# GpSimd's sums of squares wait until all eight chunks of a stage's input are split

## The reference

```python
def _rmsnorm(x, g):
    x32 = x.astype(jnp.float32)
    y = x32 * lax.rsqrt(jnp.mean(x32 * x32, axis=-1, keepdims=True) + RMS_EPS)
    return (y * g.astype(jnp.float32)).astype(x.dtype)
```

## Time and profile before

| what | value |
|---|---|
| time, median of 3 runs | 4003.52 us (4003.36 to 4012.45) |
| span of the profiled execution | 4004.4 us |
| PE busy | 3909.7 us, 98% |
| DVE busy | 2736.3 us, 68% |
| ACT busy | 1987.8 us, 50% |
| POOL busy | 212.2 us, 5% |
| mean granted clock of PE, of full speed | 0.991 |

### The profile page before, as it was taken

How to read it: one execution, slowest core, us unless ns; L and a number is a source line. 1 busy time by engine, 2 the same in 40 slices (tenths; PEclk the granted TensorE clock), 3 DMA queues, 4 the chain that set the end, 5 groups by cost and what they waited for, 6 DMA issues and landing times.

```text
span 4004.4 us, 78708 instructions
## 1 busy us (share of the span) xinstructions
PE 3909.7 (98%) x34150; PEld 3793.3 (95%) x34150; DVE 2736.3 (68%) x4071; ACT 1987.8 (50%) x2620; POOL 212.2 (5%) x277
## 2 busy tenths in 40 slices
PE   8999999999999999999999999999999999999999
PEld 8979999889998999999997999999998899999999
DVE  6566665666655656567555799956756699974855
ACT  5445444454544545465435545754444544764443
POOL 0011000110002000010023000000000000000000
PEclk9999999999999999999998999999999999999999
DMA  6534555345555455534550455456654455455754
GB/s 237 192 115 151 192 190 190 133 148 195 181 194 182 160 199 184 195 133 173 191 204 34 159 194 181 177 199 233 229 196 153 158 177 193 175 182 202 265 199 158
DMA packets 114791, 720.78 MB, mean 180 GB/s; under 512 B 13328, under 2 KB 13664, under 8 KB 32784
## 3 DMA queue, kind: packets, MB, share of 16 engines
q1 hardware_dynamic: 90144, 652.25, 45.9%
q10 hardware_dynamic: 19200, 37.01, 2.5%
q0 software_dynamic: 5104, 26.49, 1.9%
HBM read 692.48 MB, written 23.22 MB: 179 GB/s over the span
## 4 chain that ended last, share of the span: by engine, by line
PE 87%; DVE 7%; ACT 4%; issue 1%; POOL 0%; DMA 0%; ACTq 0%; DVEq 0%; POOLq 0%
PE psum L655 26%; PE psum L657 26%; PE psum L656 26%; PE psum L1408 3%; DVE slab_low L1916 2%; ACT slab_high L1427 2%; DVE h_parts L2219 1%; PE psum L1065 1%; PE psum L1048 1%; PE psum L875 1%; PE psum L1078 1%; ACT room L1670 1%; DVE room L2248 0%; DVE room L2253 0%; PE psum L1349 0%
## 5 line engine op out<-in xcount | busy, mean ns | idle before, releaser
L1916 DVE TENSOR_TENSOR slab_low<-slab,slab_high 128x2048 fp32r<-128x2048 f32 x622 | 1423.2, 2289 | 738.8 <-ACT slab_high L1427 736.6
L655 PE MATMUL psum<-h_parts,slab_high 128*128 128x256 f32 x5632 | 1578.2, 280 | 28.9 <-DVE h_parts L2219 18.6
L1427 ACT ACTIVATE slab_high<-slab 128x2048 fp32r<-128x2048 f32 x622 | 1189.3, 1912 | 785.4 <-PE psum L657 721.1
L656 PE MATMUL psum<-h_parts,slab_high 128*128 128x256 f32 x5632 | 1556.5, 276 | 0.0
L657 PE MATMUL psum<-h_parts,slab_low 128*128 128x256 f32 x5632 | 1556.1, 276 | 0.0
L655 PEld LDWEIGHTS psum<-h_parts,slab_high 128*128 128x128 f32 x5632 | 1063.5, 189 | 48.8 <-issue 24.0
L655 PE MATMUL psum<-hidden_parts,slab_high 128*128 128x256 f32 x3840 | 1063.5, 277 | 11.4 <-DVE hidden_parts L2166 4.8
L656 PEld LDWEIGHTS psum<-h_parts,slab_high 128*128 128x128 f32 x5632 | 1063.5, 189 | 2.4 <-issue 2.2
L657 PEld LDWEIGHTS psum<-h_parts,slab_low 128*128 128x128 f32 x5632 | 1062.8, 189 | 0.0
L656 PE MATMUL psum<-hidden_parts,slab_high 128*128 128x256 f32 x3840 | 1058.0, 276 | 0.0
L657 PE MATMUL psum<-hidden_parts,slab_low 128*128 128x256 f32 x3840 | 1058.0, 276 | 0.0
(11 more groups left out here) (346 smaller groups left out, 3326.0 us busy)
## 6 DMA issues: line engine op xcount, KB each, us to landing
slab<-in_up SPq DMA_DIRECT2D x176, 1024.0 KB, 4.8
slab<-in_keys_up SPq DMA_DIRECT2D x128, 1024.0 KB, 4.8
slab<-in_keys_down SPq DMA_DIRECT2D x128, 1024.0 KB, 4.8
slab<-in_down SPq DMA_DIRECT2D x88, 1024.0 KB, 4.8
slab<-in_w_in SPq DMA_DIRECT2D x16, 1024.0 KB, 4.8
slab<-in_wq SPq DMA_DIRECT2D x16, 1024.0 KB, 4.8
peer_gates<-room ACTq DMA_DIRECT2D x64, 256.0 KB, 2.3
room<-peer_gates ACTq DMA_DIRECT2D x64, 256.0 KB, 5.4
```

The source lines that it names most:

```text
L655: nc.tensor.matmul(out, lhs[0], rhs[0], start=first, stop=False, **options)
L656: nc.tensor.matmul(out, lhs[0], rhs[1], start=False, stop=False, **options)
L1427: nc.scalar.activation(k.high[m % PARTS][:, 0:width], k.slabs[m % RING][:, 0:width], ACT.Copy).then_inc(k.rounded.up())
L1916: nc.vector.tensor_tensor(k.low[m % RING][:, 0:width], k.slabs[m % RING][:, 0:width], k.high[m % PARTS][:, 0:width], ALU.subtract).then_in ...
```

## The change

GpSimd waits, once and ahead of its three additions, until `h_ready` stands at the eighth chunk of this stage. The three additions, what they read and the waits that they had stay, and so does the order of the instructions on every engine.

```diff
     def add_squares(self, v):
         k, nc = self.k, self.k.nc
+        nc.gpsimd.wait_ge(k.h_ready.sem, k.h_ready.at(DC))
         for j in range(DC // 2):
             nc.gpsimd.wait_ge(k.squared.sem, k.squared.at(j + 1))
             pair = v.square[:, 2 * j:2 * j + 2, :]
```

## The result

The changed kernel took **4035.69 us** (median of 5 executions, 4028.05 to 4038.91), the kernel before 4004.99 (median of 5 beside it): 1.007 times as long, 95% interval 1.006 to 1.008. That is +30.7 us, where +17 was forecast with 4009 to 4031 as the range: the sign was right, the size too small. Its eleven executions reach from 4020.5 to 4038.9 with a median of 4030.7, so about +25 is the better figure for what the change costs.

The account below looks back on a forecast made before the run. PE was taken to bound the kernel, with 87% of the chain. 4004.4 + 8.9 of waits (17.3 lost, 8.4 gained) + 8.2 of clock = 4021.5 us span, 0.9 less for the median: 4020.5 us, range 4009 to 4031.

Parts of the forecast that it names:

- What bounds, and what is removed: PE waiting for DVE's low parts: the eighth ready about 2.5 us sooner per stage, 8.4 us gained in four stages.
- The turns on DVE and GpSimd: Additions taking turns with DVE's slab subtractions make PE's sums late in six stages: 17.3 us lost, 6.8 in `stick`.
- PE's clock: Behind the new waits in six stages PE runs at 1.2 GHz for a while: 8.2 us lost, ends 0 and 15.
- From span to median: Whole kernel: the median lies 0.9 us below the span that was read, so 4021.5 becomes 4020.5 us.
- (1): PE's clock holds or its cost is hidden by later waits, so only the waits count: 4012.4 us, chance 0.22.
- (2): Clock costs 15 us, `mixer_one` 1.5 each, and `peer` loses its gain: 4032 us, chance 0.13.
- (3): Additions find DVE idle and sums are never late, so only the gain is left: 3995 us, chance 0.05.
- (4): Nothing happens, as additions always started after the eighth part, or gain and loss cancel: 4003.5 us, chance 0.03.

## Why the prediction was right, and where it failed

- **What bounds, and what is removed: right.** The four stages gained 8.6 us of 8.4 forecast. One sign for it was named wrongly: the idle time that low parts end was to lose most of its 18.6 us and lost 2.3. The view that groups waits tells why, of before and then of after:

```profile
PE psum L655 <- DVE h_parts L2219: 18.6, 10, 12.7
PE psum L655 <- DVE slab_low L1916: 10.0, 16, 1.2
```

```profile
PE psum L655 <- DVE h_parts L2219: 16.3, 5, 12.7
...
PE psum L655 <- DVE slab_low L1916: 3.3, 9, 1.0
```

12.7 of the 18.6 us are one wait, at the start of the program, which no edit of the stages moves; most of what fell, 6.7 us, was put down to the slab that DVE subtracts behind the low parts. The earlier trace rows names only the first releaser.
- **The turns on DVE and GpSimd: right in their sum,** 16.4 us of later sums for 17.3 forecast, `stick` to a tenth. One detail was wrong. In `stick` the addition that waited did not go ahead of DVE's next instruction, as at 17.83 in the earlier trace rows; DVE's second subtraction, back to back with the first, went ahead of it (4.48 us for two). The sum is the same in either order, so the forecast didn't notice. In `mixer_one` the middle of 0.5 to 1.5 us was taken, and 0.4 came.
- **PE's clock: the step that failed,** the term of 8.2 us with 0 and 15 as ends, where both profiles have 22. It was sized from one pair of rows, a wait of 4.8 us with half clock behind it and one of 2.0 without, by two assumptions. The first, that waits of 2 to 3.5 us lie between these, 0.7 us for each mixer, failed most: a wait of 2.4 us in the mixers cost 8.8 us for the two, nearly all of it clock, and filling brought it back to -0.6. The second, that a long wait covers part of the stretch and leaves 1.8 of 2.5 us, failed by the half: the stretch in `stick` and `fox` was 10.24 us long instead of the 6.82 read in `conv`, and cost 3.3 to 3.9 in `stick`; in `conv`, where half of the stretch lay in the wait, it cost less than forecast, 0.7. And it counted one stretch a wait, where more came in the same stages: `fox` has a second one from 3099 on, 6.8 us behind a wait of 1.7 us that had 3.4 us at half clock before, and the first mixer has four in the first profile and three in the second, where the kernel before had two. With about 17 us at the median execution (the estimate above) the term is still half of what it should be.
- **From span to median: a small step that failed.** 0.9 us was taken off; the profiled execution took 4035.69 at a span of 4034.1, 1.6 more. These pieces make the miss: 22.0 - 8.2 of clock, 7.8 - 8.9 of waits and 1.6 + 0.9 of this are 15.2 us, 4035.7 - 4020.5.
- **The rivals.** (1), the clock holds: contradicted by the trace; the kernel with all six waits filled comes near it, +12.2. (2), the upper ends, came nearest in time, but not by its mechanism: the mixers' sums and `peer` were not at their upper ends, and the clock was beyond its own in the profiled executions. (3): the additions needed their turns, as the kernel with DVE held back shows by contrast. (4): excluded as forecast, since the additions moved and the time with them. That the second measurement of the same kernel, 4027.77, lies within the range, and its fastest execution, 4020.46, on the forecast itself, is luck: it shows how wide the clock makes a kernel's times and doesn't mend the term, which is too small in both profiles.

## What to carry to other kernels

Before you let PE wait 2 us in the middle of dense work, look for what its clock does behind waits of that size in every place where there is one, not in two; price the part of the stretch that lies behind the wait at half its length, and count further stretches in the same stage. An edit that takes a collision away from one wait moves it to the next queue: make it only in the stages where that next queue has slack, which here turned +25 us into -5. Filling products that nobody needs ahead of a late result show whether a loss is the wait or the clock behind it; read it in the stage itself, since other stages' clock moves the whole by as much.

## What the runs showed of the hardware

- A wait of 2.38 us (`mixer_one`) was followed by 0.50 for 6.83 us in the midst of dense products, while one of 2.0 us in `conv` stayed at 1.00, and one of 2.2 us later in the first mixer of the kernel before has 0.50 from 0.3 us before its end. The same wait of the same stage, 2.37 us in the kernel with the additions first, was followed by 9 us at 1.00. The length of the wait alone doesn't tell.
- Stretches at half clock come and go between executions in stages whose instructions are the same: the first mixer had 10.2 us of them before and 23.9 in the kernel that leaves it untouched, at a price of 4.1 us.
- Between a GpSimd addition that waits and DVE's next two-input instruction both orders occur: in `stick` two subtractions passed it (4.48 us for both), while at 202.1 us of the changed kernel DVE's small L2044, next behind a subtraction, took 1.33 us instead of 0.18 and let it by.
